# Two-layer trunk of four mixers and key-selected experts: 36 weight chunks are copied in memory to 8 KB runs, and later loads read the copies

## What is computed

```python
pl = modulate(xl, norm1, sh1_l, sc1_l) @ w_in
a_l, b_l, m_l, h_l, gate_l = jnp.split(pl, IN_OFFSETS, axis=-1)
acc = jax.nn.sigmoid(gl[:, :, 0]) * (ys[0] @ w_branch[0])
for i in range(1, N_BRANCH):
    acc = acc + jax.nn.sigmoid(gl[:, :, i]) * (ys[i] @ w_branch[i])
return acc @ w_out
# experts: for each block of tokens, with the 128 chosen rows ib and weights gb
act = jax.nn.gelu(jnp.einsum('thkd,td->thk', u_tab[ib], hb))
return jnp.einsum('thk,thkd->td', (gb * act), v_tab[ib])
```

## Time and profile before

| | us |
|---|---|
| median of 3 runs | 3304.91 |
| lowest, highest | 3304.67, 3307.84 |
| the profiled execution | 3291.54 |
| its span, first to last instruction | 3289.6 |

### The profile page before, as it was taken

The page is one execution under the profiler, slowest core; times in us unless marked ns, Lnnn a source line. Parts: engine busy times, 40 slices in busy tenths (PEclk is TensorE's granted clock), DMA queues, the critical chain, the costliest instruction groups (busy, mean ns, idle before and its releaser), DMA issues. The chain is left out here.

```text
span 3289.6 us, 32042 instructions
## 1 busy us (share of the span) xinstructions
PE 2295.7 (70%) x10877; PEld 1373.1 (42%) x10877; DVE 1749.9 (53%) x4736; ACT 692.3 (21%) x1336; POOL 1740.7 (53%) x1580
## 2 busy tenths in 40 slices
PE   5999998778957787566777587645799455434435
PEld 2776687644524555232553155321577322101001
DVE  1202335567685556666556745573234766666662
ACT  2235532134111120211102211110442111010000
POOL 0010000467675566777676677776000577777775
PEclk8999999888667898777897588765779767555555
DMA  7677223899999999999999999998302999999997
GB/s 283 209 269 245 64 65 99 293 356 381 323 377 339 354 393 385 350 369 370 374 388 377 342 364 397 398 377 348 115 7 84 311 407 402 404 393 394 405 384 309
DMA packets 395065, 1028.54 MB, mean 313 GB/s; under 512 B 31890, under 2 KB 176282, under 8 KB 393754
## 3 DMA queue, kind: packets, MB, share of 16 engines
q0 software_dynamic: 232064, 847.35, 67.2%
q1 hardware_dynamic: 162794, 179.15, 16.3%
q10 hardware_dynamic: 48, 0.01, 0.0%
HBM read 1019.05 MB, written 7.34 MB: 312 GB/s over the span
## 5 line engine op out<-in xcount | busy, mean ns | idle before, releaser
L1942 POOL DMA_INDIRECT expert_rows<-in_peer_u,chosen x768 | 884.8, 1152 | 840.6 <-DVE chosen L2298 583.2
L2190 DVE CUSTOM_DVE_ANT_0 expert_rows<-expert_rows,h_rows 128x1024 f32<-128x1024 f32 x768 | 937.0, 1223 | 601.0 <-DMA expert_rows<-in_peer_u,chosen 580.8
L2082 PE MATMUL ps<-expert_rows,weights 128*32 128x512 f32 x3072 | 594.0, 855 | 681.3 <-DMA expert_rows<-in_peer_v,row_of 679.3
L1955 POOL DMA_INDIRECT expert_rows<-in_peer_v,row_of x768 | 826.9, 1077 | 403.9 <-PE ps L2082 200.3
L2082 PEld LDWEIGHTS ps<-expert_rows,weights 128*32 128x32 f32 x3072 | 77.2, 125 | 963.5 <-issue 953.0
L1613 PE MATMUL ps<-front,arena 128*128 128x256 f32 x1536 | 384.0, 407 | 76.5 <-DMA arena<-in_w_in 75.7
L1613 PEld LDWEIGHTS ps<-front,arena 128*128 128x128 f32 x1536 | 308.2, 205 | 163.0 <-DMA arena<-in_w_in 59.1
L654 PE MATMUL ps<-front,arena 128*128 128x256 f32 (+1 forms) x816 | 200.0, 403 | 42.6 <-DMA arena<-in_w_in 39.2
L2010 PE MATMUL ps<-h,wq 128*128 128x256 f32 x768 | 200.9, 416 | 2.4 <-ACT h L443 2.4
L654 PEld LDWEIGHTS ps<-front,arena 128*128 128x128 f32 (+1 forms) x816 | 158.6, 198 | 87.9 <-DMA arena<-in_w_in 34.3
L2010 PEld LDWEIGHTS ps<-h,wq 128*128 128x128 f32 x768 | 156.6, 211 | 55.0 <-issue 30.0
(11 more groups left out here) (360 smaller groups left out, 3159.0 us busy)
## 6 DMA issues: line engine op xcount, KB each, us to landing
arena<-in_w_in SPq DMA_DIRECT2D x79, 1024.0 KB, 14.3
arena<-in_ada_w POOLq DMA_DIRECT2D x40, 1024.0 KB, 6.6
wq<-in_peer_wq SPq DMA_DIRECT2D x48, 512.0 KB, 9.4
arena<-in_w_out SPq DMA_DIRECT2D x12, 1024.0 KB, 7.8
expert_rows<-in_peer_u,chosen POOLq DMA_INDIRECT x768, 6.6
expert_rows<-in_peer_v,row_of POOLq DMA_INDIRECT x768, 6.7
ada_w<-in_ada_w SPq DMA_DIRECT2D x4, 2048.0 KB, 23.4
arena<-in_w_branch SPq DMA_DIRECT2D x16, 512.0 KB, 3.4
```

What stands on the lines that cost most here:

```text
L1942: nc.gpsimd.indirect_dma_start(x.ring[:, j % self.R, :], None, self.u_rows, bass.IndirectOffsetOnAxis(x.chosen[:, w, q:q + 1], 0)).then_in ...
L1955: nc.gpsimd.indirect_dma_start(x.ring[:, j % self.R, :], None, self.v_rows, bass.IndirectOffsetOnAxis(x.rows[:, w % 4, 4 * c + r:4 * c + r ...
L2082: ins = nc.tensor.matmul(m.ps[to:to + 32, half, :], flat[:, r * P + 32 * c:r * P + 32 * c + 32], x.ring[:, self.place_of["v", a] % self.R, ...
L2190: nc.vector.tensor_tensor_reduce(u, u, x.ht, 1.0, 0.0, ALU.mult, ALU.add, x.dots[:, at:at + 1]).then_inc(self.u_dotted, 1)
```

## The change

`build` makes 36 buffers in memory (`kind="Internal"`), one for each chunk: 16 of layer 0's gate weights, 4 of layer 0's `w_out`, 16 of layer 1's gate weights. A new part `Relay` has GpSimd copy each chunk there, memory to memory, so that a partition's 2048 floats lie in one run. Two copies are in flight; copy i waits for copy i - 2, and the last tick waits for all. `Relay` stands in the plan of `opening` behind the parts that end the modulation, so it follows the last `ada_w` load on POOL. The gates and the output projection of the context tokens of layer 0 and the gates of layer 1, all in `experts_beside`, load from the copies. Those in `opening` and `closing` load as before.

```diff
+class Relay(Part):
+    FLIGHT = 2
+    def __init__(self, sems, copies):
+        self.copies, self.ticks = copies, len(copies)
+        self.copied = sems(*[f"copied{j}" for j in range(self.FLIGHT)])
+
+    def gpsimd(self, pool, i):
+        to, src = self.copies[i]
+        if i >= self.FLIGHT:
+            pool.wait_ge(self.copied[i % self.FLIGHT], 16 * (i // self.FLIGHT))
+        pool.dma_start(to, src).then_inc(self.copied[i % self.FLIGHT], 16)
+        if i == self.ticks - 1:
+            for j in range(self.FLIGHT):
+                pool.wait_ge(self.copied[j], 16 * len(range(j, self.ticks, self.FLIGHT)))
...
 class Gates: load
-        sp.dma_start(self.ring[:, (c + self.flip) % 2, :, 0:256], self.w[:, :, at:at + 256]).then_inc(self.ins[c % 2], 16)
+        weights = self.w[:, :, at:at + 256] if self.flat is None else self.flat[at, 256]
+        sp.dma_start(self.ring[:, (c + self.flip) % 2, :, 0:256], weights).then_inc(self.ins[c % 2], 16)
...
 class Merged: load
-        sp.dma_start(self.ring[:, c % 2, :, 0:256], self.w[:, :, c * 256:(c + 1) * 256]).then_inc(self.ins[c % 2], 16)
+        weights = self.w[:, :, c * 256:(c + 1) * 256] if self.flat is None else self.flat[256 * c, 256]
+        sp.dma_start(self.ring[:, c % 2, :, 0:256], weights).then_inc(self.ins[c % 2], 16)
...
 opening
-        plan += braid(whole(heads), g[:14], q[54:]) + [(rest0, 0), (rest1, 0)]
+        plan += braid(whole(heads), g[:14], q[54:]) + [(rest0, 0), (rest1, 0)] + whole(Relay(sems, m.copies))
...
 experts_beside: gates gets flat=m.flat_in[0], merged m.flat_out, gates_n flat=m.flat_in[1]
...
 build
+        gated = [(O_GATE + 256 * c, 256) for c in range(16)]
+        m.flat_out, m.flat_in, m.copies = {}, [{}, {}], []
+        for flats, w, wanted in ((m.flat_in[0], d["w_in"][0], gated), (m.flat_out, d["w_out"][0], [(256 * c, 256) for c in range(4)]),
+                               (m.flat_in[1], d["w_in"][1], gated)):
+            for at, n in wanted:
+                NUMBER[1] += 1
+                flat = nc.dram_tensor(f"flat{NUMBER[1]}", (P, KD * n), F32, kind="Internal").ap()
+                flats[at, n] = flat.rearrange("p (k n) -> p k n", k=KD)
+                m.copies.append((flats[at, n], w.rearrange("(k p) n -> p k n", p=P)[:, :, at:at + n]))
```

More of the change, by code:

```diff
@@ L1560, with __init__ @@
     ticks = len(STEPS) + 2
-    def __init__(self, nc, sems, m, w_in, f, ring, sig, banks, after, branches, room=None, flip=0, away=None):
-        self.away = away
+    def __init__(self, nc, sems, m, w_in, f, ring, sig, banks, after, branches, room=None, flip=0, away=None, flat=None):
+        self.away, self.flat = away, flat
         self.room_for, self.flip = room if room else [after, after], flip
@@ L1735, with __init__ @@
     ticks = KD + 1
-    def __init__(self, nc, sems, m, mod, w_out, acc, ring, lo, banks, after, room):
+    def __init__(self, nc, sems, m, mod, w_out, acc, ring, lo, banks, after, room, flat=None):
+        self.flat = flat
         self.nc, self.m, self.mod, self.acc, self.ring, self.lo, self.banks, self.after = (
@@ L2571, in experts_beside @@
         gates = Gates(nc, sems, m, d["w_in"][l], f, cut(arena, Z, 2, KD, 256), cut(arena, Z + 4096, 12, T), (4, 5),
-                      conv.done, branch)
+                      conv.done, branch, flat=m.flat_in[0])
         branch.gates = gates
@@ L2575, in experts_beside @@
                         [(branch.acc_done, len(STEPS)), (gates.mult, len(STEPS)), (gates.out, len(STEPS))],
-                        [(gates.mult, len(STEPS))])
+                        [(gates.mult, len(STEPS))], m.flat_out)
         norm2c = Norm(nc, sems, m, mod, 3 * KD, 0, h2, cut(arena, 2048, T), 6,
@@ L2592, in experts_beside @@
         gates_n = Gates(nc, sems, m, d["w_in"][l + 1], f, cut(arena, Z, 2, KD, 256), cut(arena, Z + 4096, 12, T), (4, 5),
-                        heads_n.done, None, away=sigs)
+                        heads_n.done, None, away=sigs, flat=m.flat_in[1])
         conv_n = Hyena(nc, sems, m, vec, d, f, hyena_memory(arena, 0, Z), spectra, (4, 5, 6),
```

## The result

The changed kernel takes 3264.91 us (median of 4 runs, 3255.75 to 3276.63); the kernel before, run beside it, 3306.38 us. The ratio is 0.9871 (95% interval 0.9833 to 0.9909): 41 us less, where 19 were forecast. The time lies inside the range, near its lower end, which had been set for rival 3; the direction was right, the size forecast was half of what came.

A forecast was written before the change was run, and what follows sets the result against it. Transfers were taken to bound the expert stage, TensorE the rest of the opening. Chunks -16, waits -8 and copies +5 gave -19 us: from a median of 3304.9 to about 3286 us, range 3260 to 3322.

The forecast's parts named there:

- rival 3: Expert stage: 0.93 us saved a chunk, all three gaps closed, copies done early; -51.5 us, 3253 us; chance 0.12.
- What bounds the stage: Expert stage, 600 to 2280 us: transfers are the bound at share 0.99, so engine time saved should come off the time.
- What a chunk saves, -16 us: Expert stage: 8 KB instead of 1 KB runs save 0.45 us of engine time a chunk, 16 us for 36.
- The end of 34 us: Upper end of the chunk saving, from chunks loaded alone: 0.93 us saved each, 34 us for all.
- What the waits give, -8 us: Gate stretches: faster landing shortens TensorE's waits, recovering half of 17.5 us of lost engine time, 8 us.
- three windows of 10 us: Behind the three longest TensorE waits, transfer share falls to 0.61, 0.26 and 0.50: 17.5 us of engine time.
- What the copies cost, +5 us: Opening's tail: copies running to 508 us slow `w_branch` and `w_out` loads; 5 us taken, 19 us the most.
- the formula: Opening: copies end at 306 + 67 + 36 T, with T us of engine time a copy.
- 1 (the copies outlast the opening): GpSimd's final wait before the barrier: copies run past 565 us, kernel slower; +44 us at 7.0 us a copy; chance 0.20.
- T: Opening: microseconds a copy takes; 4.3 taken, ends 3.0 and 7.0; gain used up at 5.8.
- 2 and 4 (nothing to see): Expert stage: no visible gain, 3302 us, chance 0.15; or loads don't come as 8 KB runs, 3310 us, chance 0.03.
- The likeliest case: Whole kernel: the forecast itself, -19 us, about 3286 us, own range 3272 to 3298; chance 0.50.

The follow-up runs named there:

- The unread loads: Changed kernel plus 15 loads of 512 KB in 4 KB runs that nobody reads, beside layer 1's gates: 3283.46 us, ratio 0.995.
- unused copies: Changed kernel with all 36 copies made but every load reading the original weights: 3302.11 us, ratio 1.000.
- short runs: Changed kernel with each row padded by 16 floats in the copies, so loads read them in 1 KB runs: 3306.09 us, ratio 1.0028.
- 72 copies: Changed kernel with 36 more copies behind the 36, into buffers that nobody reads: 3291.5 us, ratio 0.9985.

## Why the prediction was right in direction and half in size

- **What bounds the stage** (an engine-microsecond comes off the time): right. The unread loads were paid 20 to 23 us for 19, of which up to 5.8 could be ScalarE's waits.
- **What a chunk saves, -16 us**: right. By the queue rows of the first gate stretch (below) SP's queue took 26.1% of 237 us, 61.9 us of all engines, before, and 24.4% of 218, 53.2 us, after; in the second 24.1% of 253, 61.0, and 22.4% of 237, 53.1. That is 16.6 us for 32 chunks, 0.52 each, where 0.45 was taken; the two full rates gave 15. The rule that the Trainium skill gives ("DMA: Bandwidth & Descriptors", Specifications) for line rate, 512 B or more, would have made this 0; runs of 1 KB and 8 KB differ here, 393 against 406 GB/s, and the measurement decides. The end of 34 us, from chunks loaded alone, was not met. That 0.45 came so near is in part luck: the 8 KB price was read from a window without gathers in which `sigs` was not alone. Of its 1171 packets 752 are under 8 KB (first line below), as a load of `w_branch` shares the window, so `sigs` has 3.4 of the 4.74 MB. Behind that line the queues of the first gate stretch, before and after:

```profile
DMA packets 1171, 4.74 MB, mean 395 GB/s; under 512 B 112, under 2 KB 112, under 8 KB 752
```

```profile
q0 software_dynamic: 17920, 65.24, 71.2%
q1 hardware_dynamic: 19632, 20.97, 26.1%
```

```profile
q0 software_dynamic: 18381, 66.94, 77.5%
q1 hardware_dynamic: 5447, 21.28, 24.4%
```

- **What the waits give, -8 us: this is the step that failed.** Landing fell to 8.1 us, at the upper end of what was said, and the waits to 11.4, but the term was mis-sized by three: the pauses closed are some 23 us in the gate stretches, and the `w_out` stretch got 6 us shorter where its chunks' engine time is 2. Two choices made it small. The first, worth 9 us, was to take half of the 17.5 us that three windows of 10 us showed, since "only its landing shrinks, by about half of the wait". The three waits did shrink by about half (12.9 to 6.2, 14.2 to 5.2, `w_branch` 10.7 to 5.8), but the pauses behind them did not halve, they went: behind a wait of 6.2 us the slices of after show 404 and 416 GB/s where those of before show 102 and 312. The second, worth some 6 us in the gate stretches, was "shorter waits elsewhere in these stretches are worth nothing to me": the eight short ones of the second gate stretch were worth 2 to 5 us, windows of 10 us cut the dips short, and the waits for `w_out` were in no window of mine. Comparing the stretch's mean rate with its full rate, 365 against 393 GB/s over 237 us, would have shown 17 us in the first gate stretch alone, on the rows of before.
- **What the copies cost, +5 us**: the path was wrong, the size is not refuted. From 306 to 456 us GpSimd's queue took 73.3% of 150 us after and 2.5% before, so (0.733 - 0.025) x 150 / 36 = 2.95 us a copy: the lower bound, reading and writing overlap fully. With it the formula gives 459 us for the end; it was near 457, not 508. That queue's rows, before and after:

```profile
q0 software_dynamic: 331, 1.22, 2.5%
q0 software_dynamic: 10101, 38.91, 73.3%
```

  The Trainium skill ("DMA: Bandwidth & Descriptors", Latency and other measured facts) has 207 to 214 GB/s each way for rows of 16 KB; 1.049 MB in 2.95 us are 355 GB/s each way, so the prediction's end of 549 us, estimated from that figure, was not met either. So the tail was not slowed: TensorE waits there for `w_branch` 1.0 us at most. What the copies slowed are the opening's gate loads (landing 11.6 us, 5.2 before), and TensorE waits for one of them, 2.1 to 3.5 us in each of the seven profiles with 36 copies and not at all in the two without. The opening ends 1 us later in the profile after, but that pair lies at the favourable end: from the last `ada_w` load to TensorE's last L523 the seven take 260.5 to 271.4 us (mean 264.0), the two without copies 259.2 and 257.7. By these, some 5 us; the two longest also had a lower granted clock (0.95 and 0.88 of full speed from 456 to 500 us, where most had 1.00), and the whole runs, 0 with unused copies and 9 with short runs, each give or take 9, don't decide.
- **Rivals.** 1 (the copies outlast the opening) did not come, as T was 2.95 and not 5.8, and is real at 72 copies. 2 and 4 (nothing to see) fall with the windows and the landing. 3 (a larger gain) came in size for a reason half its own: the gaps closed, but not the 0.93 us a chunk. The likeliest case should have taken its gaps and left its chunks: with the `w_out` stretch's 6 us less the 2 that are in the 16 already, -16 - 23 - 4 + 5 = -38, 3267 us, 2 from the result. This sum is made from the measured terms and tests nothing.

## What to carry to other kernels

Where gathers with 4 KB packets share the transfer engines with weight loads in 1 KB runs, the short runs cost twice: a little engine time for each load, and a long landing that lets the consumer stall. Value the second from the whole stretch (its mean rate against its own full rate, times its length), not from half of the deepest dips and not from the sum of the waits: here 23.6 us of two long waits cost 13.8 us, 24 us of eight short ones 2 to 5. Repacking is worth its bytes where the transfers idle for long enough, and the count that fits there follows from one copy's engine time. Set a stage against itself in several profiles before calling its cost nothing: one pair of openings said 1 us, nine said 5.

## What the hardware showed that I had not expected

- A copy within memory cost the engines no more than a load of the same 1 KB runs (2.95 us against 3.02 for 1.049 MB), beside other loads, at a transfer share of 0.98.
- With the 1 KB packets gone, the gathers beside them also became cheaper: by the rows of q0 above 71.2% of 237 us for 65.24 MB before, 2.59 us a MB, and 77.5% of 218 us for 66.94 MB after, 2.52.
- The last experts stage, with identical instructions, took 711.6 to 728.3 us in eleven profiles. The profile shown before has its shortest, so two spans alone would have understated the gain by 13 us.
